# Routed encoder layer on one core: expert choice from two sorted halves, with most top-k rounds inside the token tiles' steps

## The reference, cut to what matters

```
x = x + gate1 * mix
h2 = rms_norm(x, norm2_g) * (1 + scale2) + shift2
aff = softmax(h2 @ w_router)              # n tokens x 16 experts
g, idx = top_k(aff.T, cap)                # cap = 2 n / 16: 64 (prompt), 128 (sample)
xe = h2[idx]
ye = (silu(xe @ w_gate) * (xe @ w_up)) @ w_down * g
y  = x + gate2 * zeros.at[idx].add(ye)
```

## Time and profile before

| | us |
|---|---|
| median of 3 runs | 3413.82 (3413.45 to 3413.94) |
| the profiled execution's own time | 3411.49 |
| its span, first to last instruction | 3409.3 |
| TensorE busy (matmul) | 3169.9 |
| VectorE busy | 2298.9 |
| ScalarE busy | 1911.0 |
| mean granted clock of TensorE | 0.965 of 2.4 GHz |

### The profile page before, as it was taken

One profiled execution on the slowest core, in us unless ns is written; L12 is line 12 of the kernel. 1 busy time (PEld: TensorE's weight loads), 2 busy tenths in 40 slices (PEclk: granted clock), 3 DMA queues, 4 the chain that ended last, 5 costly groups with the idle time before them and its releaser, 6 DMA issues.

```text
span 3409.3 us, 50511 instructions
## 1 busy us (share of the span) xinstructions
PE 3169.9 (93%) x18950; PEld 2832.9 (83%) x18950; DVE 2298.9 (67%) x3457; ACT 1911.0 (56%) x3096; POOL 150.8 (4%) x209
## 2 busy tenths in 40 slices
PE   5999877798099999999999999999999999999997
PEld 3777654587089999999999999999999999999997
DVE  4678815633757776767677776767677676767675
ACT  5143435655056666666666665666666666666654
POOL 0000000000000100101010010101010010101000
PEclk8999988999589999999999999999999999999999
DMA  8321137232345766657575765757576665757572
GB/s 308 130 62 53 47 100 248 104 131 93 146 178 218 264 231 241 241 201 275 193 288 218 251 237 226 254 206 277 194 273 226 241 250 221 263 187 278 210 253 87
DMA packets 136261, 690.67 MB, mean 203 GB/s; under 512 B 12032, under 2 KB 39824, under 8 KB 112528
## 3 DMA queue, kind: packets, MB, share of 16 engines
q1 hardware_dynamic: 125824, 659.68, 51.9%
q0 software_dynamic: 7168, 25.17, 3.2%
q10 hardware_dynamic: 3088, 3.10, 0.3%
HBM read 650.14 MB, written 37.77 MB: 202 GB/s over the span
## 4 chain that ended last, share of the span: by engine, by line
PE 72%; DVE 2%; DMA 0%; POOL 0%; ACT 0%; issue 0%; POOLq 0%; DVEq 0%
PE psG L1318 32%; PE psG L1320 15%; PE psY L1334 5%; PE psY L1337 5%; PE psY L1335 5%; PE psY L1336 5%; PE psY L1338 5%; DVE idxu L1508 1%; DVE affT L1510 1%; DVE vals L1506 1%; PE psG L1285 0%; PE psG L1286 0%; DMA xg_s<-xhat_d,inow 0%; ACT xst L1417 0%; DVE xe L1529 0%
## 5 line engine op out<-in xcount | busy, mean ns | idle before, releaser
L1318 PE MATMUL psG<-xe,w_gu_hi_part 128*128 128x384 f32 x5632 | 1630.8, 360 | 4.2 <-DVE xe L1529 4.2
L1320 PE MATMUL psG<-xe,w_gu_lo_part 128*128 128x192 f32 x5632 | 1411.3, 251 | 0.0
L1320 PEld LDWEIGHTS psG<-xe,w_gu_lo_part 128*128 128x128 f32 x5632 | 1076.9, 191 | 7.9
L1318 PEld LDWEIGHTS psG<-xe,w_gu_hi_part 128*128 128x128 f32 x5632 | 1058.9, 188 | 12.6 <-DVE xe L1529 4.6
L1519 DVE TENSOR_TENSOR w_gu_lo_part<-raw_gu,w_gu_hi_part 128x1024 fp32r<-128x1024 f32 x704 | 858.8, 1222 | 117.8 <-ACT w_gu_hi_part L1428 117.8
L1428 ACT ACTIVATE w_gu_hi_part<-raw_gu 128x1024 fp32r<-128x1024 f32 x704 | 741.2, 1055 | 13.1 <-DMA raw_gu<-in_w_gu 13.1
L1553 DVE TENSOR_TENSOR gu<-psG,low 128x384 f32<-128x384 f32 x352 | 195.7, 556 | 569.3 <-ACT low L1458 569.3
L1524 DVE TENSOR_TENSOR w_dn_lo_part<-raw_dn,w_dn_hi_part 128x1024 fp32r<-128x1024 f32 x352 | 431.0, 1224 | 0.5 <-ACT w_dn_hi_part L1439 0.5
L1458 ACT ACTIVATE low<-psG 128x384 f32<-128x384 f32 x352 | 172.0, 489 | 417.0 <-PE psG L1320 417.0
L1439 ACT ACTIVATE w_dn_hi_part<-raw_dn 128x1024 fp32r<-128x1024 f32 x352 | 367.7, 1045 | 0.8 <-PE psY L1338 0.8
L1417 ACT ACTIVATE xst<-psG,modv,a 128x128 f32<-128x128 f32 (+1 forms) x256 | 95.7, 425 | 392.2 <-PE psG L1320 325.4
(11 more groups left out here) (161 smaller groups left out, 3185.3 us busy)
## 6 DMA issues: line engine op xcount, KB each, us to landing
raw_gu<-in_w_gu SPq DMA_DIRECT2D x176, 2048.0 KB, 7.9
raw_dn<-in_w_down SPq DMA_DIRECT2D x176, 1024.0 KB, 8.8
shared<-in_ada_w SPq DMA_DIRECT2D x12, 2048.0 KB, 9.7
bias<-in_bias SPq DMA_DIRECT2D x8, 1536.0 KB, 12.3
w_raw<-in_w_in SPq DMA_DIRECT2D x20, 512.0 KB, 5.6
qk_d<-shared SPq DMA_DIRECT2D x8, 768.0 KB, 3.8
qk<-qk_d SPq DMA_DIRECT2D x8, 768.0 KB, 11.5
out<-wo_raw SPq DMA_DIRECT2D x12, 512.0 KB, 2.6
```

Source lines behind the costliest of these rows:

```text
L1318: pe.matmul(bank[:, 0:2 * CAP], wh, xe[:, k, :, :].rearrange("p a b -> p (a b)"), start=(k == 0), stop=False, skip_group_check=True)
L1320: mm = pe.matmul(bank[:, 0:CAP], wl, xe[:, k, 0, :], start=False, stop=(k == KD - 1), skip_group_check=True)
```

## The change

The top 128 of the sample's 1024 tokens are found as two sorted lists of 128, one of each half of 512 tokens, and merged: with the second list reversed, the larger of each pair of values belongs to the top 128. `affT` becomes 80 x 512: the prompt in rows 0 to 15, the sample's second half in rows 32 to 47, its first half in rows 64 to 79. `mix` takes the sample's eight tiles first (first half, second half), then the prompt's four. When a half is complete, its rounds are dealt into the later steps' VectorE lists at three places: after the normalization, before the wait for the exponential, and at the end of the step. 16 rounds of the first half and 8 of the second go there; 8 rounds over rows 0 to 47 (prompt and the rest of the second half) follow at the end of `mix`. In `experts` the reversal is a matmul with a reversed identity (`flip`, a new input), and a few VectorE operations merge. Besides, in `front`, `ident` is loaded over SP behind the first x tile, TensorE's first wait is for it and the conditioning alone, and the scaling of `qkg` moves behind tile 5. The core of the diff (what follows from the new order, `MIX_ORDER[t]` in place of `t` in the loads, stores and splits, is left out):

```diff
+def routed_set(tile):
+    return 0 if group(tile) == 0 else 2 - (tile * P - PROMPT) // (SAMPLE // 2)
...
-        affT = sb(g, "affT", [48, SAMPLE])
+        affT = sb(g, "affT", [80, SAMPLE // 2])
+        vals = sb(g, "vals", [80, CAP_S])
+        idxu = sb(g, "idxu", [80, CAP_S], U32)
...
-        CONSTS = 16 * (5 + CG)
+        CONSTS = 16 * (4 + CG)
...
                 load_x(0)
+                sp.dma_start(ident[:, :], A["ident"]).then_inc(c_loaded, 16)
                 load_x(1)
...
-                pe.wait_ge(consts, CONSTS)
+                pe.wait_ge(c_loaded, 48)
                 turn_x(0)
...
-                act.dma_start(ident[:, :], A["ident"]).then_inc(consts, 16)
...
-                act.wait_ge(c_loaded, 32)
+                act.wait_ge(c_loaded, 48)
...
-                dve.wait_ge(consts, CONSTS)
-                dve.tensor_scalar(qkg[:, 0:1], qkg[:, 0:1], DH ** -0.5, None, ALU.mult).then_inc(qkg_ready, 1)
...
                     if t == 5:
+                        dve.wait_ge(consts, CONSTS)
+                        dve.tensor_scalar(qkg[:, 0:1], qkg[:, 0:1], DH ** -0.5, None, ALU.mult).then_inc(qkg_ready, 1)
                         ada_rows(0)
...
+MIX_ORDER = list(range(PROMPT // P, TILES)) + list(range(PROMPT // P))
+HALF_TILES = SAMPLE // 2 // P
+ROUNDS_AT = {6: (0, 0, 1), 7: (1, 1, 1), 8: (1, 1, 2), 9: (1, 1, 2), 10: (1, 1, 2), 11: (1, 1, 2), 12: (1, 1, 1), 13: (0, 1, 0)}
...
-                load_conv(0)
+                load_conv(1)
...
-                        pe.transpose(psL[0:48, 1, 0:P], af[:, t % 2, :], ident[:, :]).then_inc(aff_t, 1)
+                        pe.transpose(psL[0:80, 1, 0:P], af[:, t % 2, :], ident[:, :]).then_inc(aff_t, 1)
...
+                def top_round(rows, r):
+                    sl8 = slice(8 * r, 8 * r + 8)
+                    n = done[0]
+                    if n:
+                        dve.wait_ge(top_d, n)
+                    dve.max(vals[rows, sl8], affT[rows, :]).then_inc(top_v, 1)
+                    dve.wait_ge(top_v, n + 1)
+                    dve.max_index(idxu[rows, sl8], vals[rows, sl8], affT[rows, :]).then_inc(top_i, 1)
+                    dve.wait_ge(top_i, n + 1)
+                    dve.match_replace(affT[rows, :], vals[rows, sl8], affT[rows, :], -2.0).then_inc(top_d, 1)
+                    done[0] += 1
+
+                def rounds(s, place):
+                    for _ in range(ROUNDS_AT.get(s, (0, 0, 0))[place]):
+                        if done[0] < ROUNDS:
+                            if done[0] == 0:
+                                dve.wait_ge(aff_out, HALF_TILES)
+                            top_round(slice(64, 80), done[0])
+                        else:
+                            if done[0] == ROUNDS:
+                                dve.wait_ge(aff_out, 2 * HALF_TILES)
+                            top_round(slice(32, 48), done[0] - ROUNDS)
...
                         dve.tensor_scalar(xh[:, t % 2, :], xt[:, t % XR, :], st[:, 3, t:t + 1], None, ALU.mult).then_inc(xh_ready, 1)
+                        rounds(s, 0)
...
                         dve.tensor_scalar(lg[:, 1, t % 2:t % 2 + 1], lg[:, 0, t % 2:t % 2 + 1], -1.0, None, ALU.mult).then_inc(l_neg, 1)
+                        rounds(s, 1)
                         dve.wait_ge(l_exp, t + 1)
...
-                        if t == 4 or t == 5:
-                            dve.memset(af[:, t % 2, 0:EXPERTS], 0.0)
...
+                        dve.tensor_copy(affT[at:at + EXPERTS, col:col + P], psL[at:at + EXPERTS, 1, 0:P]).then_inc(aff_out, 1)
+                    rounds(s, 2)
+
+                dve.wait_ge(aff_out, TILES)
+                for r in range(ROUNDS - CAP_P // 8, ROUNDS):
+                    top_round(slice(0, 48), r)
...
+                sp.dma_start(flip[:, :], A["flip"]).then_inc(gate_loaded, 16)
                 for grp in range(2):
                     sp.dma_start(gate2[:, grp, :], ada_d[grp:grp + 1, 5 * D:6 * D].to_broadcast([P, D])).then_inc(gate_loaded, 16)
...
-                pe.wait_ge(top_v, ROUNDS)
-                pe.transpose(psG[:, 0, 0:48], vals[:, :], ident[0:48, 0:48]).then_inc(tT_done, 1)
+                pe.transpose(psG[:, 0, 0:80], vals[:, :], ident[0:80, 0:80]).then_inc(tT_done, 1)
                 pe.wait_ge(idx_f, 1)
-                pe.transpose(psG[:, 1, 0:48], idxf[:, :], ident[0:48, 0:48]).then_inc(tT_done, 1)
+                pe.transpose(psG[:, 1, 0:80], idxf[:, :], ident[0:80, 0:80]).then_inc(tT_done, 1)
+                pe.wait_ge(gate_loaded, 48)
+                pe.wait_ge(merged, 1)
+                pe.matmul(psG[:, 2, 0:96], flip[:, :], top[:, :, 0:48], start=True, stop=True).then_inc(flipped, 1)
...
-                for r in range(ROUNDS):
...
                 dve.tensor_copy(idxf[:, :], idxu[:, :]).then_inc(idx_f, 1)
                 dve.wait_ge(tT_done, 2)
-                dve.tensor_copy(gsel[:, :], psG[:, 0, 0:48])
-                dve.tensor_scalar(iall[:, :], psG[:, 1, 32:48], float(PROMPT), None, ALU.add)
-                dve.tensor_copy(isel[:, :], psG[:, 1, 0:48]).then_inc(sel_ready, 1)
+                dve.tensor_copy(top[:, :, :], psG[:, 0:2, 0:80]).then_inc(merged, 1)
+                dve.wait_ge(merged, 1)
+                turned = psG[:, 2, 0:96].rearrange("p (a e) -> p a e", a=2)
+                first, second = top[:, :, 64:80], turned[:, :, 32:48]
+                dve.wait_ge(flipped, 1)
+                dve.tensor_copy(gsel[:, 0:EXPERTS], turned[:, 0, 0:EXPERTS])
+                dve.tensor_copy(isel[:, 0:EXPERTS], turned[:, 1, 0:EXPERTS])
+                dve.tensor_tensor(keep[:, 0, :], first[:, 0, :], second[:, 0, :], ALU.is_ge)
+                dve.tensor_tensor(gsel[:, 32:48], first[:, 0, :], second[:, 0, :], ALU.max)
+                dve.tensor_scalar(keep[:, 1, :], second[:, 1, :], float(SAMPLE // 2), None, ALU.add).then_inc(merged, 1)
+                dve.wait_ge(merged, 2)
+                dve.tensor_tensor(keep[:, 2, :], first[:, 1, :], keep[:, 1, :], ALU.subtract).then_inc(merged, 1)
+                dve.wait_ge(merged, 3)
+                dve.tensor_tensor(keep[:, 2, :], keep[:, 2, :], keep[:, 0, :], ALU.mult).then_inc(merged, 1)
+                dve.wait_ge(merged, 4)
+                dve.tensor_tensor(keep[:, 1, :], keep[:, 1, :], keep[:, 2, :], ALU.add).then_inc(merged, 1)
+                dve.wait_ge(merged, 5)
+                dve.tensor_scalar(iall[:, :], keep[:, 1, :], float(PROMPT), None, ALU.add)
+                dve.tensor_copy(isel[:, 32:48], keep[:, 1, :]).then_inc(sel_ready, 1)
```

More of the change, by code:

```diff
@@ L129, in program @@
             attend(nc, A, sem, sb, ps, qk_d, v_d, ident, attn)
-            mix(nc, A, sem, sb, ps, rows_of, x_d, y_d, ada_d, conv_d, xhat_d, ident, eps_col, modv, a2, affT, attn)
-        experts(nc, A, sem, sb, ps, y_d, ada_d, xhat_d, ident, modv, a2, affT)
+            mix(nc, A, sem, sb, ps, rows_of, x_d, y_d, ada_d, conv_d, xhat_d, ident, eps_col, modv, a2, affT, vals, idxu, attn)
+        experts(nc, A, sem, sb, ps, y_d, ada_d, xhat_d, ident, modv, a2, vals, idxu)
 Z_TILES = [("gate", 0), ("value", 0), ("gate", 1), ("value", 1), ("q", 0), ("q", 1), ("q", 2),
@@ L452, in side @@
                     else:
+                        pe.wait_ge(consts, CONSTS)
                         pe.wait_ge(ada_row, MODS)
@@ L950, in _, with mix @@
                                        psT[:, :, 0:n * P].rearrange("p w (m q) -> p w m q", q=P), ACT.Copy).then_inc(pT_out, 1)
-def mix(nc, A, sem, sb, ps, rows_of, x_d, y_d, ada_d, conv_d, xhat_d, ident, eps_col, modv, a2, affT, attn):
+MIX_ORDER = list(range(PROMPT // P, TILES)) + list(range(PROMPT // P))
+HALF_TILES = SAMPLE // 2 // P
+ROUNDS_AT = {6: (0, 0, 1), 7: (1, 1, 1), 8: (1, 1, 2), 9: (1, 1, 2), 10: (1, 1, 2), 11: (1, 1, 2), 12: (1, 1, 1), 13: (0, 1, 0)}
+def mix(nc, A, sem, sb, ps, rows_of, x_d, y_d, ada_d, conv_d, xhat_d, ident, eps_col, modv, a2, affT, vals, idxu, attn):
     XR = 3
+    ROUNDS = CAP_S // 8
+    top_v, top_i, top_d = sem("top_vals"), sem("top_idx"), sem("top_drop")
     conv_loaded = [sem(f"conv_loaded{i}") for i in range(NCH)]
@@ L1005, in _ @@
                     if s == 1:
-                        for n in range(1, NCH):
+                        for n in (2, 0):
                             load_conv(n)
@@ L1225, in experts @@
         gate2 = sb(c, "gate2", [P, 2, D])
-        vals = sb(c, "vals", [48, CAP_S])
-        idxu = sb(c, "idxu", [48, CAP_S], U32)
-        idxf = sb(c, "idxf", [48, CAP_S])
+        idxf = sb(c, "idxf", [80, CAP_S])
+        flip = sb(c, "flip", [P, P])
+        top = sb(c, "top", [P, 2, 80])
+        keep = sb(c, "keep", [P, 3, EXPERTS])
         gsel = sb(c, "gsel", [P, 48])
@@ L1579, in _ @@
                 dve.wait_ge(sel_ready, 1)
-                dve.wait_ge(gate_loaded, 32)
+                dve.wait_ge(gate_loaded, 48)
                 for i in range(AHEAD):
```

51 lines of the change are left out of this document (23 added, 28 removed).

## The result

The changed kernel takes 3514.11 us (3510.97 to 3516.92, four runs) against 3413.64 for the kernel before on the same chip: 1.0296 times as long, 95% interval 1.0281 to 1.031. The forecast was 3400.6 and its range 3386 to 3410. The profiled execution took 3510.97 us.

What follows compares the result with a forecast made beforehand. A line of stages bounds the kernel: selection leaves TensorE waiting 90.8 us, then TensorE's loop, taken as unchanged. Terms -40.8 + 22.8 + 8.4 - 3.6 = -13.2 from 3411.5 give 3398.3, plus 2.3 for the median: 3400.6 us, range 3386 to 3410.

Steps and rivals of the forecast that it cites:

- The slower rival that I gave 0.05: Pauses in `mix` keep TensorE at 1.2 GHz through whole steps: +37 us, 3438 us; chance 0.05.
- front: Start of the kernel: waiting for `ident` alone closes a DMA pause, 3.6 us less, ends 0 and 9.
- dealt rounds and clock: Steps of `mix`: 24 dealt rounds delay by 22.8 us, TensorE's lower clock after pauses adds 8.4.
- last copy to first gate-up: From the last copy into `affT` to the first gate-up matmul: 50.0 us instead of 90.8, 40.8 less.
- first gate-up matmul: Its start moves by the sum of all terms, -13.2 us.
- step 10: Step of `mix` ending with two rounds: 0.98 us of slack, so 3.6 us, plus 2.1 for the clock.
- the tail: Last steps of `mix`: rounds in step 12 cost 0.6 us and in step 13 1.9.
- full DMA engines from 22 us on: Front: DMA stays full from 22 us until the projection, so only 3.6 us of unused DMA time is gained.
- the matmul waited for `gate2`: After the rounds, the reversal matmul waits for both `gate2` loads: 4.6 us to landing, T + 5.5 with issue.
- POOL's copies: After the rounds: four copies take 0.7 us, bounds 0.7 and 4.6, since weight splits come later.
- the gather: After the rounds: gather to turn stays 10.9 us, 10.64 of it the transfer.
- The rival that the gather waits behind the ring loads: After the rounds: the gather, served only behind the ring's 8 MB, lands 6.2 us later; 3407 us, chance 0.1.

Runs made afterwards that it cites:

- a_unroll: The changed kernel with VectorE's loop over experts 1 to 14 written out, so it never jumps back: 3395.03 us, ratio 0.995 to the kernel before.
- the last experiment: The kernel with fewer dealt rounds, joint rounds of 80 rows and written-out loop (3374.66 us), given a separate semaphore for `flip`: 3372.52 us.
- the two runs that remove them: The changed kernel with 39 memsets that compute nothing in attention, 3395.04 us, and the changed kernel with VectorE's expert loop written out, 3395.03 us.
- the run with the longer body: The kernel before with 78 one-column memsets ahead of VectorE's expert loop (3412.9 us), plus 30 memsets inside that loop (289 instructions instead of 259): 3426.4 us.

## Why the prediction was wrong, point by point

**The step that failed** is the sentence that opens the argument: "From 950 on the chain is TensorE's in nearly every piece, and the change leaves that loop alone." The code of the loop is the same, but its place in VectorE's list isn't. Of an edit ahead of a loop I counted the time of every instruction, and not that 89 of them move the loop to a start from which it is fetched anew at every jump. That is +117.4 us. The rows of before could not have shown the pause, for there is none in them. The three things that go into it were within reach: a hardware loop on VectorE, 2459 of 3409 us spent while it runs, and a change in the number of instructions ahead of it. They deserved a rival with its price left open and a few per cent of chance (of the nine starts tried two pause, and these two are one place in a packet), not none.

The slower rival that I gave 0.05 (TensorE at 1.2 GHz through whole steps of `mix`) did not happen: the steps grew by 2 to 7 us. That the kernel came out slower is no merit of that rival: the mechanism was another.

**The other steps, to the first gate-up matmul:**

| term | forecast | in the trace |
|---|---|---|
| front | -3.6 | -4.9 (projection 60.10 for 64.99); -3.0 in `a_unroll` (61.98); alone -3.8 |
| dealt rounds and clock | +22.8 + 8.4 = 31.2 | +27.3 |
| last copy to first gate-up | 50.0 instead of 90.8 | 50.8 (881.49 to 932.32) |
| first gate-up matmul | -13.2 | -17.6 |

The middle row is 881.49 - 651.31 = 230.2 us from the start of `mix` to the last copy, where before it was 202.9. Step by step, growth forecast against growth found in the gaps of the turns, each against the same gap before (14.2 to 14.3 us; 13.7 at step 10, 12.7 at step 11): behind step 6, 1.9 and 2.1; 7, 1.9 + 1.05 and 2.5; 8, 4.2 + 1.05 and 4.3; 9, 4.2 + 2.1 and 6.5; 10, 3.6 + 2.1 and 3.7; 11, 4.6 + 2.1 and 6.6; the tail, 2.5 and 2.0 (866.50 to 881.49 against 12.95 before). Only step 10 is off by more than 1 us. In `a_unroll`, with the same rounds, steps 10 and 11 grew by 4.8 and 4.5 us (turns at 832.51, 850.92 and 868.09), and the turn at 850.92 was at the full clock, so part of this split is where the clock happens to fall in one execution. Taken together rounds and clock were put 4 us too high. The clock did fall after pauses of the length I had named, and did come back. The Trainium skill (TensorE: Matmul & The Clock Gate, section "HAM oscillation — how this bites in real kernels") has the return paid again in each pass of such a loop; here the expert loop with its 13 pauses is that case, and each cost about 2.3 us of clock (the estimate above).

Two readings need a word. POOL's copy alone stands at 0.18 us in the earlier trace rows, not 0.17. And the page's slices are 85 us wide and can't show full DMA engines from 22 us on; windows of 5 us do (0.99 and more from 25 to 70 us in the kernel before).

From the last copy to gate-up: the rounds were 2.29 us apart as forecast; the matmul waited for `gate2` (6.27 us of transfer in the chain where I had 4.6 plus issue); POOL's copies were at 0.18 us as soon as no weight splits ran beside them, as in the late row; the gather took 10.04 us. The rival that the gather waits behind the ring loads did not come in the changed kernel, but the last experiment shows its mechanism once the gather starts 5 us sooner.

So without the pauses the sum stands, 5.6 us too high: 3395.04 and 3395.03 us in the two runs that remove them against 3400.6, inside the range.

**What the chip does** at the jump is shown only from outside. The Trainium skill (Runtime: NRT & Kernel Launch, section "Instruction fetch mechanics") says that instructions are streamed through a small buffer ahead of the engine, in blocks of 16 KB or 256 instructions, and that a jump to a target no longer in its window of two blocks has to fetch it first. The traces agree that a jump back may stall, by 10.3 us here, with about five packets (66 / 13) fetched per pass; they disagree on the block, since this queue's packets are of 8 KB and the pausing place repeats after 128 instructions (the packets of q8 are of 2.49 MB / 152 = 16 KB). That touching a fourth packet decides is the account that foretold the one run that the others did not; it is not proved. What the pause would be with idle DMA engines is open too: they were busy in the pauses looked at (0.98 between 1244 and 1248.5 us in the changed kernel, 1.09 between 1262.3 and 1265.4 in the run with the longer body), and nothing else was tried.

## What to carry to other kernels

An edit ahead of a hardware loop in VectorE's list is an edit of that loop (for the other engines' loops this was not tried). Before a change is judged, look in both profiles for idle time with no releaser at the loop's first instruction, once per pass, and for the packet count of the instruction queue; if it is there, shift the loop by a few dozen instructions or write it out on that engine, and judge the change then (here 2.96% slower became 0.5% faster).

Work dealt into waits on an engine is free where the wait is longer than the work (steps of 14.33 us with two rounds and without), and paid nearly in full, with the clock on top, at the end of the loop. With the rounds of most steps kept in the waits, the joint ones widened to all 80 rows and VectorE's loop written out, the kernel takes 3374.66 us, 1.1% less than before; with a semaphore of its own for `flip` it is 3372.52, the best here.

## What the runs showed of the hardware that was not expected

- A pause of 10.3 us at the head of a VectorE loop of 259 instructions at every jump, at two of nine starts tried, which are 128 instructions apart; none at the other seven.
- Around each of these jumps four packets of 8 KB come over the instruction queue, three of them in the pause; without the pause the queue is empty for 2000 us of the loop.
- 39 memsets that compute nothing took 119 us off a kernel.
- A loop in a good place is as fast as the written-out one (3395.04 and 3395.03 us).
- A top-8 round takes the same 2.3 us for 48 and for 80 rows of 512 columns; at 1024 columns it was 3.90.
- A gather issued 5 us sooner, while the weight ring is being filled, took 5 us longer (14.31 for 9.36).
